# Six of the twelve conditioning column blocks summed by VectorE instead of GpSimd

## What is computed

```python
# first block, its second half
x = x + jnp.concatenate([out_a, out_b, out_m], axis=-1) @ w_out[l]
x = x + conv_ffn(rms_norm(x, ffn_norm_g[l]), w_up[l], conv_w[l], conv_b[l], w_down[l])
# second block
c_act = jax.nn.silu(c)
mod = c_act @ w_ada[l] + b_ada[l]                     # (1, 6144)
sh1, sc1, g1, sh2, sc2, g2 = jnp.split(mod, 6, axis=-1)
h = rmsnorm(x, norm1_g[l]) * (1.0 + sc1[:, None, :]) + sh1[:, None, :]
proj = h @ w_in[l]
...
x = x + g1[:, None, :] * (merged @ w_out[l])
h2 = rmsnorm(x, norm2_g[l]) * (1.0 + sc2[:, None, :]) + sh2[:, None, :]
x = x + g2[:, None, :] * hierarchical_moe(h2, ...)
```

## Time and profile before

| | us |
|---|---|
| device time, median of 3 runs | 1189.49 |
| the three runs | 1183.27, 1189.49, 1189.81 |
| device time of the profiled execution | 1185.82 |
| its span, first to last instruction | 1183.3 |
| VectorE busy | 566.4 (48%) |
| GpSimd busy | 212.8 (18%) |
| mean granted TensorE clock | 0.902 of full |

### The profile page before, as it was taken

The page is one execution under the profiler, slowest core; times in us unless marked ns, Lnnn a source line. Parts: engine busy times, 40 slices in busy tenths (PEclk is TensorE's granted clock), DMA queues, the critical chain, the costliest instruction groups (busy, mean ns, idle before and its releaser), DMA issues.

```text
span 1183.3 us, 19004 instructions
## 1 busy us (share of the span) xinstructions
PE 953.8 (81%) x8281; PEld 735.5 (62%) x8281; DVE 566.4 (48%) x955; ACT 346.8 (29%) x680; POOL 212.8 (18%) x177
## 2 busy tenths in 40 slices
PE   3999999999888889899999987957675767575765
PEld 2786777479788868798889986534342434242432
DVE  2453577358999996677665653211111111111113
ACT  2331154235555553545554323100000100010101
POOL 3105210026766765520000010000000000000000
PEclk9998899889898899999998897978787978887979
DMA  9332564056555557543334487999999999999994
GB/s 314 118 116 105 207 216 144 1 181 202 174 191 168 206 186 244 192 169 116 143 143 147 151 311 312 426 428 426 427 429 426 426 429 427 426 427 428 428 426 196
DMA packets 77897, 314.58 MB, mean 266 GB/s; under 512 B 3504, under 2 KB 27217, under 8 KB 61297
## 3 DMA queue, kind: packets, MB, share of 16 engines
q1 hardware_dynamic: 72512, 296.43, 63.4%
q0 software_dynamic: 4704, 15.17, 4.2%
q10 hardware_dynamic: 592, 1.71, 0.4%
HBM read 312.24 MB, written 1.06 MB: 265 GB/s over the span
## 4 chain that ended last, share of the span: by engine, by line
PE 49%; DMA 26%; DVE 17%; ACT 4%; issue 2%; ACTq 1%; SPq 1%; DVEq 0%
PE ps L447 47%; DMA w<-in_w_up 25%; DVE sp L1725 8%; DVE ub L1816 2%; DVE ub L1814 2%; ACT sp L1716 1%; DMA w<-in_w_in 1%; ACTq L2655 1%; SPq L2643 1%; PE ps L505 1%; DVE ub L1819 1%; DMA rows<-in_mem_k_norm 1%; PE ps L2415 0%; PE ps L1975 0%; DVE ht L1747 0%
## 5 line engine op out<-in xcount | busy, mean ns | idle before, releaser
L447 PE MATMUL ps<-hb,sp 128*128 128x256 f32 x1824 | 241.8, 294 | 23.7 <-DVE sp L1725 21.5
L447 PEld LDWEIGHTS ps<-hb,sp 128*128 128x128 f32 x1824 | 231.6, 198 | 32.7 <-DVE sp L1725 23.2
L447 PE MATMUL ps<-w,xg 128*32 128x256 f32 x2048 | 157.4, 475 | 113.6 <-DMA w<-in_w_up 105.8
L1725 DVE TENSOR_TENSOR sp<-w,sp 128x1024 fp32r<-128x1024 f32 x122 | 187.5, 1575 | 39.2 <-ACT sp L1716 39.0
L447 PEld LDWEIGHTS ps<-w,xg 128*32 128x32 f32 x2048 | 87.5, 136 | 183.7 <-issue 163.2
L1716 ACT ACTIVATE sp<-w 128x1024 fp32r<-128x1024 f32 x122 | 121.9, 1049 | 43.9 <-PE ps L447 32.5
L2540 DVE TENSOR_TENSOR hh<-ps,sgl 64x256 f32<-64x256 f32 x32 | 13.6, 426 | 227.4 <-ACT sgl L2480 227.4
L2480 ACT ACTIVATE sgl<-ps 64x256 f32<-64x256 f32 x32 | 12.1, 378 | 337.4 <-PE ps L447 337.4
L2559 DVE TENSOR_TENSOR ost<-ps,g2q 32x256 f32<-32x256 f32 x128 | 53.8, 420 | 111.4 <-PE ps L447 108.4
L836 POOL TENSOR_TENSOR w<-w,cpad 128x512 f32<-128x512 f32 x48 | 74.7, 1577 | 85.6 <-DMA w<-in_w_ada 85.6
L447 PE MATMUL ps<-w,hts 128*32 128x256 f32 x1024 | 68.0, 410 | 13.0 <-ACT hts L2496 11.4
(11 more groups left out here) (365 smaller groups left out, 1242.5 us busy)
## 6 DMA issues: line engine op xcount, KB each, us to landing
w<-in_w_down SPq DMA_DIRECT2D x37, 2048.0 KB, 22.2
w<-in_w_gate SPq DMA_DIRECT2D x32, 2048.0 KB, 27.8
w<-in_w_up SPq DMA_DIRECT2D x32, 2048.0 KB, 32.3
w<-in_w_in SPq DMA_DIRECT2D x14, 2048.0 KB, 8.3
w<-in_w_up SPq DMA_DIRECT2D x22, 1024.0 KB, 7.7
w<-in_w_ada SPq DMA_DIRECT2D x6, 2048.0 KB, 9.3
w<-in_w_out SPq DMA_DIRECT2D x4, 2048.0 KB, 8.6
w<-in_w_ada POOLq DMA_DIRECT2D x10, 768.0 KB, 5.0
```

The source lines that it names most:

```text
L447: return q.eng.matmul(o, l, r, start=start, stop=stop, skip_group_check=True)
L1725: q.eng.tensor_tensor(w[1][:, ks, :], src[:, ks, :], w[0][:, ks, :].bitcast(F), SUB).then_inc(s["split"], 1)
```

## The change

Chunks 6 and 7 become VectorE's whole-chunk work (`ada_ve`), right after the recurrence and its gates: chunk 6, the output projection's first sum, chunk 7, the second sum. They are loaded whole by SyncE's queue into slot 2 and into slot 6 (a region that the first block's attention used, hence two waits), ahead of the up weights. Their accumulators are a pair outside the slots; TensorE sums them ahead of the up projection, and `mods_ve` takes the result.

Chunks 8 to 11 stay in slot 1 and are loaded in three groups of rows (3, 3, 2) by GpSimd's queue, but VectorE multiplies and sums them (`ada_late_ve`), one group at a time: after the splits of halves 26, 28, 30 and 32 in `down_ve`, and at pieces 3, 11, 19 and so on to 59 of `proj2_ve`. GpSimd only issues loads, each after VectorE used the group before.

The up weights rotate over slots 2, 0 and 1; the late weights after them have slots 0 and 2 swapped.

```diff
@@ slots
-            return (s["ada_d"], 8 * i) if 0 < i < NVEC else (s["ada_k"], 15 * max(i - 4, 1))
+            return (s["ada_d"], 8 * i) if i else (s["ada_k"], 15)
-                                      (0, (("out", 0), ...)), (1, (("out", 1), ...))]:
+                                      (0, (("out", 0), ...)), (1, (("out", 1), ...)), (2, ada(6)), (6, ada(7))]:
         for i, (name, parts) in enumerate(late):
-            place(name, 1 if name == ("out2", 1) else 2 - 2 * (i % 2), *parts)
+            if i == 11:
+                for n in range(8, 12):
+                    chunks["ada", n] = Chunk(("ada", n), [ada_rows(n, a, b) for a, b in ADA_ROWS], 1, held[1], (s["ada_w"], 48 * (n - 7)))
+                    held[1] = ("ada", n)
+            place(name, (2, 0, 1)[i % 3] if i < 11 else 1 if name == ("out2", 1) else 2 * (i % 2), *parts)
@@ the late chunks
         def ada_late_gp(q, i):
+            ch = chunks["ada", i]
+            for z, (a, b) in enumerate(ADA_ROWS):
+                dst, src = ch.parts[z]
+                q.wait_ge(*(used(ch.before) if i == 8 and z == 0 else (s["ada_d"], 8 * i - 8 + a)))
+                q.eng.dma_start(dst(ch.ap), src).then_inc(ch.tok[0], 16)
+
+        def ada_late_ve(q):
+            for i in range(8, 12):
+                ch, o = chunks["ada", i], lacc_of(i)
+                for z, (a, b) in enumerate(ADA_ROWS):
+                    w = ch.parts[z][0](ch.ap)
+                    q.wait_ge(ch.tok[0], ch.tok[1] - 16 * (2 - z))
+                    for k in range(a, b):
+                        if k == 0:
+                            q.eng.tensor_scalar(o, w[:, 0, :], cpv[:, 0, 0:1], None, MUL).then_inc(s["ada_d"], 1)
+                        else:
+                            q.wait_ge(s["ada_d"], 8 * i - 8 + k)
+                            q.eng.scalar_tensor_tensor(out=o, in0=w[:, k - a, :], scalar=cpv[:, k, 0:1], in1=o, op0=MUL, op1=ADD).then_inc(s["ada_d"], 1)
+                    yield
@@ down_ve, proj2_ve
             for j in range(25, 33):
                 split_ve(q, j)
+                if j > 25 and j % 2 == 0:
+                    next(late_ada)
...
+                if g % 8 == 3:
+                    next(late_ada, END)
@@ TensorE's sums, SyncE's waits
         def mods2_pe(q):
-            b = take(q, 6)
-            for i in (6, 8):
-                adapair_pe(q, i, b[:, 4 * i - 24:4 * i - 16])
+            adapair_pe(q, 8, take(q, 6)[:, 0:8])
...
+                if ch.slot_no == 6:
+                    q.wait_ge(*((s["r_n"], 8) if ch.name[0] == "ada" else (s["mg_lo"], 4)))
+                    q.wait_ge(s["a1_c"], NA)
@@ the streams
             weave(rwkv_ve(q), beside_ve(q))
+            for i in (6, 7):
+                for _ in ada_ve(q, i):
+                    pass
+                wout_ve(q, 0, (i - 6,))
             norm_ve(q, 2, x, xn1, hs=(0,))
...
             feat_pe(q, 2, xn1, ft2, hs=(1,))
+            adapair_pe(q, 6, psum[7][:, 16:24])
+            free[7] = [(s["ada"], 4)]
             up_pe(q)
```

More of the change, by code:

```diff
@@ L239, in block_kernel @@
         ysq = sb("ysq", RB + 9216, 384)
-        acc = [sb(f"acc{i}", o, 512) for i, o in enumerate((43568, 52384, 44080, 47264, 47776, 48288))]
+        acc67 = sb("acc67", 51376, 1024)
+        acc = [sb(f"acc{i}", o, 512) for i, o in enumerate((43568, 52400, 44080, 47264, 47776, 48288))]
+        acc += [acc67[:, 0:512], acc67[:, 512:1024]]
         xn1 = sb("xn1", RB + 8192, 2048)
@@ L252, in block_kernel @@
         ht2 = sb("ht2", 49312, 2048)
-        junk2 = sb("junk2", 51360, 1024)
-        lacc = slot[1][:, 1536:4096]
+        lacc = slot[1][:, 1536:3584]
         Q = [sb(f"q{i}", 36000 + 1024 * i, 1024) for i in range(6)]
@@ L377, in block_kernel @@
                                       (2, ada(0)), (0, ada(1)), (2, ada(2)), (0, ada(3)), (1, ada(4)), (2, ada(5)),
-                                      (0, (("out", 0), wcols(w_o, 0, 512))), (1, (("out", 1), wcols(w_o, 512, 512)))]:
+                                      (0, (("out", 0), wcols(w_o, 0, 512))), (1, (("out", 1), wcols(w_o, 512, 512))), (2, ada(6)), (6, ada(7))]:
             place(name, slot_no, part)
-        ADA_ROWS = {i: ((0, 3), (3, 6), (6, 8)) if i < 11 else ((0, 2), (2, 4), (4, 6), (6, 8)) for i in range(6, 12)}
+        ADA_ROWS = ((0, 3), (3, 6), (6, 8))
         def ada_rows(i, a, b):
             return lambda sl: v(sl[:, 0:512 * (b - a)], b - a), w_ada[128 * a:128 * b, 512 * i:512 * i + 512].rearrange("(k p) n -> p k n", p=128)
[L386 to L389, removed]
         ORD2 = (2, 0, 1, 3, 4, 5, 6, 7, 8, 9)
@@ L811, in ada_ve @@
                 q.wait_ge(s["rq_mm"], 3)
-            elif i > 2:
+            elif i in (3, 4, 5):
                 q.wait_ge(s["qp"], 6)
@@ L819, in ada_ve @@
                 yield
+        ADA_LATE = [("ada", i) for i in range(8, 12)]
         def lacc_of(i):
-            return lacc[:, 512 * (i - 6):512 * (i - 6) + 512] if i < 11 else slot[1][:, 1024:1536]
-        ADA_LATE = [("ada", i) for i in range(6, 12)]
+            return lacc[:, 512 * (i - 8):512 * (i - 8) + 512]
         def ada_late_gp(q, i):
[L828 to L846, removed]
@@ L1606, in wout_pe, with wout_ve @@
                 yield
-        def wout_ve(q, h):
-            for c in range(2):
+        def wout_ve(q, h, cs=(0, 1)):
+            for c in cs:
                 o = x[:, h, 512 * c:512 * c + 512]
@@ L1682, in beside_ve @@
                 yield
-            for _ in range(4):
-                yield
-            wout_ve(q, 0)
         def weave(lead, other):
@@ L1873, in mods_ve @@
         def mods_ve(q):
-            q.wait_ge(s["ada_sum"], 6)
+            q.wait_ge(s["ada_sum"], 7)
             q.eng.tensor_tensor(modc[:, 0:16], psum[7][:, 0:16], col("b_ada_2", 0, 16), ADD).then_inc(s["ada"], 1)
+            q.wait_ge(s["par2"], N_PAR2)
+            q.eng.tensor_tensor(modc[:, 16:24], psum[7][:, 16:24], pk[:, 8:16], ADD).then_inc(s["ada"], 1)
             q.wait_ge(s["ada"], 3)
@@ L1888, in mods2_ve @@
             q.wait_ge(s["ada_sum"], 9)
-            q.wait_ge(s["par2"], N_PAR2)
-            for z in range(2):
-                q.eng.tensor_tensor(modc[:, 16 + 8 * z:24 + 8 * z], psum[6][:, 8 * z:8 * z + 8], pk[:, 8 + 8 * z:16 + 8 * z], ADD).then_inc(s["ada"], 1)
+            q.eng.tensor_tensor(modc[:, 24:32], psum[6][:, 0:8], pk[:, 16:24], ADD).then_inc(s["ada"], 1)
             q.wait_ge(s["gb"], 80)
@@ L2048, in proj2_sc, with proj2_ve @@
                     split_sc(q, 35 + g // 4)
-        def proj2_ve(q):
+        def proj2_ve(q, late_ada):
             e = q.eng
@@ L2683, in _ @@
             split_sc(q, 1)
-            norm_sc(q, 2, x, rdy2, junk2, (1,))
+            norm_sc(q, 2, x, rdy2, psum_all[:, 2048:3072], (1,))
             hi_sc(q, 2, ht2, hb, "ft2", 1, (1,))
@@ L2751, in _ @@
             up_ve(q)
-            down_ve(q)
+            late_ada = ada_late_ve(q)
+            down_ve(q, late_ada)
             xffn_ve(q, 0)
@@ L2762, in _ @@
             split_ve(q, 35)
-            proj2_ve(q)
+            proj2_ve(q, late_ada)
             mix_ve(q)
@@ L2791, in _ @@
                 e.memset(v(u, 4)[:, :, 0:2], 0.0).then_inc(s["u_z"], 1)
-            for i in range(6, 12):
+            for i in range(8, 12):
                 ada_late_gp(q, i)
```

9 lines of the change are left out of this document (4 added, 5 removed).

## The result

| | before | after |
|---|---|---|
| device time, median | 1188.47 (1183.27 to 1189.81, 4 runs) | 1141.08 (1136.97 to 1155.24, 4 runs) |
| span of the profiled execution | 1183.3 | 1153.4 |

The account below looks back on a forecast made before the run. TensorE's up projection was taken to wait for VectorE's low parts, slowed by GpSimd's late chunks; DMA bounds the experts. Terms -31.2 - 4.5 - 2.1 + 0.5 + 1.5 - 3.9 = -39.7 from 1189.5 give 1149.8, forecast 1150, range 1141 to 1157.

Parts of the forecast that it names:

- A: Up projection: TensorE no longer waits for low parts slowed by GpSimd, 129.7 us instead of 160.9, -31.2.
- B: Down projection: TensorE's 5.0 us of idle time mostly goes, the four row groups on VectorE stay hidden; -4.5.
- C: Join: two slowed VectorE operations on the chain to TensorE's next full stretch return to quiet length; -2.1.
- F's clock: Late sums: with fewer short matmuls the clock would perhaps not fall to half; another -4 us, not counted.
- E: Second input projection: eight row groups on VectorE, mostly in its idle time; +1.5, bounds 0 and 18.4.
- F: Late sums: `mods2_pe` loses one of two pairs, 16 of the 32 records that take 7.77 us; -3.9.
- The rival that the ScalarE-VectorE trip sets the pace: Up projection: hand-overs make the round trip about 12.7 us per chunk, 12 us more, 1162; chance 0.15.
- D: Chunks 6 and 7 beside the output projection: 16 more short TensorE records ahead of the up projection; +0.5, bounds 0.1 and 1.7.
- The experts and the loads: Experts' start: first load about 13 us later through the slot swap, but hidden; without that, up to 5.1 us.
- The rival that they land late: Row groups: loads land late and VectorE's splits wait behind them; 1235 if landing took 25 us; chance 0.04.
- The rival that GpSimd isn't the cause: Up projection to join: GpSimd isn't what slows VectorE, L1725 keeps its lengths, no relief, 1188; chance 0.05.

Follow-up runs that it names:

- the new order: Kernel after, with VectorE writing the accumulators of chunks 6 to 9 in the order in which TensorE reads them as weights; 1137.20 us, ratio 0.958.

## Why the prediction was right, step by step

The mechanism, its place and the stages to which it reaches were right: A, B and C have the sign and nearly the size forecast, the rest is near nothing.

That the time lies in the range is in part luck. 1141.1 is 8.7 us under the 1149.8 of the sum and 0.1 above the lower bound. Of the two reasons given for that bound, F's clock (4) and E at nothing (1.5) lead to 1144.3 only. And the absolute time hangs on how often the head is long: a second set of four runs has 1149.3. The ratio does not hang on it: 0.960 and 0.963, where the sum says 0.967.

Over the first traces the sum is -48.5 instead of -39.7, over the second -43.4. A, B and C together are -42.2 and -42.7, where I had -37.8. That part of the miss is real, and the other terms but F are within the spread.

- **A, -33.7 for -31.2.** The term that was mis-sized is the pace of TensorE, 5.83 us per half, taken from one stretch of two halves. The long run of 720 matmuls (15 halves in 85.70 us) has 5.71. 22 halves at 5.71 and 1.6 for the slow start are the 127.2 measured; the allowance for the start (1.4) was right. The rival that the ScalarE-VectorE trip sets the pace didn't come true: TensorE isn't idle once. ScalarE waited 14.9 us for TensorE, in the list of waits, and VectorE 16.9 for ScalarE, so the three buffers for halves are full.
- **B, -5.4 for -4.5.** TensorE is busy for all 62.38 us. The 5.0 us of idle time that I read in a window of 68 us hold a part of the join; the stage itself, of 67.74 us, had 4.5, and all of it is gone. What I left out is that TensorE also needs 0.8 us less for its matmuls (63.20 before). The fourth row group is hidden by the wait of L1870, as said.
- **C, -3.1 for -2.1.** The two slowed operations are at 2.35 and 0.69 us, and bring what I counted. The other 1.0 is more than the 0.4 that I named and left out, and it is the clock. Before, TensorE waited 2.82 us for the low part, ran at a granted clock of 0.67 to 0.71 from 489.4 to 495 us, and its transposes, for which VectorE waits next, took 1.91 us. After, it waits 1.78 us and stays at full clock:

```profile
489.42 2.25 PE L447 MATMUL ps<-sp,hb 128*128 128x256 f32 x12 [2.82 <-DVE sp L1725]
491.47 1.91 PE L505 MATMUL ps<-cst,xn 128*128 128x128 f32 x8
```
```profile
467.45 1.70 PE L448 MATMUL ps<-sp,hb 128*128 128x256 f32 x12 [1.78 <-DVE sp L1723]
468.98 1.04 PE L506 MATMUL ps<-cst,xn 128*128 128x128 f32 x8
```

- **D, -0.5 for +0.5.** The 16 records took 3.86 us, the upper bound of my two, not 2.3: they read every eighth column, the 32 of the earlier trace rows at that place don't. TensorE's 2.17 us of idle time ahead of the up projection are gone against them. The second trace has 38.28 for the stage, the second of before 35.31; nothing finer can be said of D than between -0.5 and +3, which is wider than my bounds of 0.1 and 1.7, and a kernel without most of the VectorE work of these chunks has the same 38.28. Chunks 6 and 7 cost nothing, by that run.
- **E, +0.2 for +1.5.** It is -1.5 over the second traces, so nothing near the upper bound. That bound was too high: the eight groups have 21 rows, not 24, and took 15.2 us, not 18.4. They are covered by idle time, and the run with more VectorE work shows that the cover is nearly used up: 7.3 us for 13.9 us of busy time more.
- **F, -5.1 for -3.9.** The 16 records are -3.8 (3.96 for 7.77). The rest, 1.3 us, is the half clock, which lasted 7.6 us less. I had named up to 4 for it and not counted it; a third of that came.
- **The experts and the loads**: 452.2 for 452.1 us, as forecast; no wait of VectorE or TensorE for a row group's load stands in the lists of waits from the down projection on. The rival that they land late fell: they take 4.9 us to land in the median.

The rival that GpSimd isn't the cause is refuted from both sides, by its removal before and its return after. What stays open is why the head of the kernel is granted different clocks from run to run (from 180 to 200 us 1.00 in one trace, 0.77 to 0.80 in others). The medians can't tell effects of less than about 10 us for that reason.

## What to carry to other kernels

Where an engine that isn't the bound does cheap background work, ask what it does to the instructions beside it: compare the duration of one operation of one shape, with the neighbour idle and with it busy, within one trace. If VectorE feeds TensorE with operations of two SBUF operands, GpSimd's arithmetic is the wrong place for late work even when it is free there; the idle gaps of VectorE itself cost less, as long as its hand-overs stay on time (78% busy cost nothing here, 83% cost 7.3 us). Price a wait of TensorE together with the granted clock after it: about a third of A, and of C, was TensorE at a lower clock, not TensorE waiting. A gain in pace should be sized by the longest uninterrupted stretch in the trace, not by a short one.

## What was unexpected of the hardware

- The price of GpSimd's products on TensorE's stage isn't linear: 0.40 us each for the first 24, 0.97 for the next 24. That the halves split ahead make the difference is argued from the timeline, not tested.
- One-column matmuls whose weights come at a step of eight f32 elements took 0.25 us each (16 in 3.96 us at clock 1.00), those with neighbouring columns 0.12 (16 in 1.95 at 1.00, and 32 in 3.63 at 1.00). At the half clock the stepped ones were no slower (16 in 3.86 at 0.58), the others were (16 in 3.41 at 0.50). So here the step, not the clock, sets the time of the first kind, and the gain of the new order is large only where the clock is full.
- The clock fell to half with TensorE at work without a gap: in the kernel before TensorE was busy for all 13.6 us at a granted 0.51, and the fall, at 643.7 us, lies in the run of 32 one-column matmuls (from 639.99). With 16 of them it came 1.2 us after the last, and the half clock lasted 6.0 us.
